# Norms pipelined by pairs of tiles in a two-block transformer kernel

## The reference

```python
# first block: mixer with adaLN, 32 experts of which each token takes 4
x = x + g1 * (mixed @ w_out)
h2 = rms_norm(x, norm2_g) * (1 + sc2) + sh2
x = x + g2 * moe_ffn(h2, ...)
x = rms_norm(x, final_g)
# second block, two layers
x = layer_norm_2(x, ln_emb_g, ln_emb_b)
for layer in range(2):
    mix = hybrid_mixer(x, ...)                      # attention + two-way retention
    x = layer_norm_2(ALPHA * x + mix, ln1_g[layer], ln1_b[layer])
    ffn = swiglu(x, ...) if layer == 0 else moe_swiglu(x, ...)   # 8 experts, 2 a token
    x = layer_norm_2(ALPHA * x + ffn, ln2_g[layer], ln2_b[layer])
```

## Time and profile before

| | us |
|---|---|
| median of 3 runs | 2596.67 (2596.26 to 2632.82) |
| the profiled execution | 2595.71 |
| its span | 2594.0 |
| PE busy | 2352.8 (91%) |
| DVE busy | 705.4 (27%) |
| ACT busy | 550.8 (21%) |
| POOL busy | 300.4 (12%) |

### The profile page before, as it was taken

How to read it: one execution, slowest core, us unless ns; L and a number is a source line. 1 busy time by engine, 2 the same in 40 slices (tenths; PEclk the granted TensorE clock), 3 DMA queues, 4 the chain that set the end, 5 groups by cost and what they waited for, 6 DMA issues and landing times.

```text
span 2594.0 us, 35046 instructions
## 1 busy us (share of the span) xinstructions
PE 2352.8 (91%) x13496; PEld 1499.8 (58%) x13497; DVE 705.4 (27%) x1313; ACT 550.8 (21%) x784; POOL 300.4 (12%) x129
## 2 busy tenths in 40 slices
PE   4999799999999999999949997999799869999996
PEld 3877644444444434444429876998698655444443
DVE  5854323222222222322251322010222331111013
ACT  1132011212112111111215811420266001111111
POOL 1000000000000000000017412660363000000000
PEclk8999889999999999999979988999899879999998
DMA  9942369999999999989924415444442436799560
GB/s 371 369 161 100 81 258 418 418 417 417 418 418 418 418 417 417 416 346 417 402 65 147 114 49 162 131 162 130 142 134 82 187 130 267 299 407 398 230 267 16
DMA packets 226021, 688.58 MB, mean 265 GB/s; under 512 B 31290, under 2 KB 120194, under 8 KB 190114
## 3 DMA queue, kind: packets, MB, share of 16 engines
q1 hardware_dynamic: 221472, 685.81, 69.0%
q10 hardware_dynamic: 4482, 1.81, 0.3%
HBM read 686.53 MB, written 1.05 MB: 265 GB/s over the span
## 4 chain that ended last, share of the span: by engine, by line
PE 72%; DMA 10%; SPq 8%; DVE 6%; issue 1%; ACT 1%; ACTq 0%; DVEq 0%
PE PS L876 15%; PE PS L624 13%; PE PS L633 11%; DMA RAW<-in_w_exp_in 9%; PE PS L977 7%; SPq L425 6%; PE PS L840 4%; PE PS L988 3%; PE PS L1156 3%; PE PS L673 2%; PE PS L859 2%; PE PS L941 2%; SPq L447 1%; PE PS L647 1%; PE PS L887 1%
## 5 line engine op out<-in xcount | busy, mean ns | idle before, releaser
L876 PE MATMUL PS<-RAW,Z 128*64 128x512 f32 x3168 | 715.0, 598 | 24.6 <-DMA RAW<-in_w_exp_in 23.8
L876 PEld LDWEIGHTS PS<-RAW,Z 128*64 128x64 f32 x3168 | 214.2, 137 | 456.1 <-issue 377.2
L377 POOL TENSOR_TENSOR WLO_D<-W,WHI_D 128x2048 fp32r<-128x2048 f32 x60 | 277.5, 4626 | 1364.3 <-ACT WHI_D L374 1364.3
L977 PE MATMUL PS<-W,Z 128*64 128x384 f32 (+1 forms) x1408 | 216.9, 465 | 7.4 <-DMA W<-in_moe_w 6.1
L633 PE MATMUL PS<-Z,W 128*128 128x256 f32 x768 | 177.0, 394 | 20.1 <-DVE Z L1980 12.3
L633 PEld LDWEIGHTS PS<-Z,W 128*128 128x128 f32 x768 | 151.6, 198 | 45.3 <-DVE Z L1980 13.8
L977 PEld LDWEIGHTS PS<-W,Z 128*64 128x64 f32 x1408 | 100.0, 138 | 125.4 <-issue 67.6
L624 PE MATMUL PS<-XHI,WHI_D 128*128 128x256 f32 x880 | 128.7, 290 | 29.2 <-ACT XHI L1353 19.5
L374 ACT ACTIVATE WHI_D<-W 128x2048 fp32r<-128x2048 f32 x60 | 114.1, 1904 | 177.0 <-DMA W<-in_w_in 91.5
L624 PEld LDWEIGHTS PS<-XHI,WHI_D 128*128 128x128 f32 x880 | 116.0, 196 | 37.6 <-ACT XHI L1353 20.3
L840 PE MATMUL PS<-Z 128*128 128x64 f32 x1088 | 128.6, 278 | 3.1 <-DVE Z L1763 3.1
(11 more groups left out here) (336 smaller groups left out, 2199.6 us busy)
## 6 DMA issues: line engine op xcount, KB each, us to landing
RAW<-in_w_exp_in SPq DMA_DIRECT2D x256, 1024.0 KB, 19.3
RAW<-in_w_exp_out SPq DMA_DIRECT2D x128, 1024.0 KB, 21.8
W<-in_moe_w SPq DMA_DIRECT2D x128, 704.0 KB, 15.1
W<-in_w_in SPq DMA_DIRECT2D x52, 1024.0 KB, 6.1
W<-in_moe_w SPq DMA_DIRECT2D x40, 1024.0 KB, 14.3
W<-in_ffn_w SPq DMA_DIRECT2D x33, 1024.0 KB, 5.3
W<-in_w_ada SPq DMA_DIRECT2D x24, 1024.0 KB, 13.0
W<-in_w_out SPq DMA_DIRECT2D x12, 1024.0 KB, 5.0
```

Of the source, the lines that this page charges most:

```text
L377: eng.tensor_tensor(lo, raw, hi.bitcast(F32), ALU.subtract).then_inc(sem("dense_lo"), 1)
L876: mm = pe.matmul(ps(bank, 512, 64 * h, 64 * h + 64), x, w[:, c:c + 512], start=first, stop=final, skip_group_check=True)
L977: mm = pe.matmul(ps(2 * i + b, n, 64 * h, 64 * h + 64), X1[:, s, :], first2(s)[:, c:c + n], start=(s == 0), stop=(s == 7), skip_group_chec ...
```

## The change

- **Layer norm in one pass by pairs** (`shift_sum`, `moments`, `normalised`, `shifted_parts`). The mean over the first 256 features is a shift that is taken off all tiles; then PE sums x and x^2 of each pair of tiles when DVE has it, and the variance is mean(x^2) - mean(x)^2. The sums of the first pairs stand between the jobs of `w_out`, or behind the last slot of ffn2. DVE scales by pairs, and ACT applies gain and bias with one instruction a tile, which writes XHI directly; then X again.
- **`first_jobs`**: the first two split jobs behind a norm do all work with XHI, tile by tile as pairs arrive, then all with XLO.
- **Final rms norm and embedding layer norm made one**: XW is X times final_g; its mean and variance and the sum of X^2 give one root, of var + EPS * mean(x^2) + EPS^2.
- **The ends of the experts**: X takes what Y holds before the last scatters, which go to different banks (`scatter_last`) and are added straight to X.
- **`route`**: logits and transposes alternate tile by tile as pairs arrive.
- **Head norm and mixed sum** by pairs; the product with the silu gate is put ahead of the wait for the head sums.
- **The output** is transposed, copied (by ACT and DVE) and stored in four pieces. The square root's table is loaded ahead (`root_table`), and the two expert stages share semaphores.

The core of the diff:

```diff
+            def first_jobs(lin):
+
+
+                n = ("qa0", "ffn1", "qa1").index(lin.name)
+
+                def split(q, buf):
+                    return buf[:, q % SPLIT_N, :].rearrange("p (k n) -> p k n", k=KT)
+
+                for s in range(2):
+                    q = split_ready(lin, s)
+                    job = lin.job0 + s
+                    bank_free(job)
+                    for k in range(KT):
+                        if s == 0 and k % 2 == 0:
+                            pe.wait_ge(sem("stream_hi"), 4 * n + k // 2 + 1)
+                        for j in range(2):
+                            for i, w in enumerate((WHI_D, WLO_D)):
+                                pe.matmul(ps(job % 2, T, c0=j * T), split(q, w)[:, k, j * P:(j + 1) * P], XHI[:, k, :],
+                                          start=(i == j == k == 0), stop=False, skip_group_check=True)
+                for s in range(2):
+                    q = split_ready(lin, s)
+                    job = lin.job0 + s
+                    for k in range(KT):
+                        if s == 0 and k % 2 == 0:
+                            pe.wait_ge(sem("stream_lo"), 4 * n + k // 2 + 1)
+                        for j in range(2):
+                            mm = pe.matmul(ps(job % 2, T, c0=j * T), split(q, WHI_D)[:, k, j * P:(j + 1) * P], XLO[:, k, :],
+                                           start=False, stop=(k == KT - 1), skip_group_check=True)
+                    mm.then_inc(sem("lin_done"), 1)
...
+            def shift_sum(src, b):
+
+                for k in range(2):
+                    mm = pe.matmul(ps(b, T), ONES[:, :], src[:, k, :], start=(k == 0), stop=(k == 1))
+                mm.then_inc(sem("norm_sum"), 1)
+
+            def moments(src, squares, p, first, last, b1, b2):
+
+
+                def total(bank, c0, x):
+                    for k in (2 * p, 2 * p + 1):
+                        mm = pe.matmul(ps(bank, T, c0=c0), ONES[:, :], x[:, k, :],
+                                       start=(first and k == 2 * p), stop=(last and k == 2 * p + 1))
+                    if last:
+                        mm.then_inc(sem("norm_sum"), 1)
+
+                norm[0] += 1
+                if not last:
+                    pe.wait_ge(sem("norm_in"), norm[0])
+                total(b1, 0, src)
+                pe.wait_ge(sem("norm_in"), norm[0])
+                total(b2, T, squares)
...
                 scatter(count, 0)
-                scatter(count, 1)
+                scatter_last("m1")
+                pe.wait_ge(sem("xw_ready"), 1)
+                shift_sum(XW[:, 0:2, :], 1)
+                for i, p in enumerate((0, 2, 1)):
+                    moments(XW, XWSQ, p, i == 0, False, 3, 1)
+                pe.wait_ge(sem("x_squared"), 1)
+                for k in range(KT):
+                    mm = pe.matmul(ps(0, T), ONES[:, :], H[:, k, :], start=(k == 0), stop=(k == KT - 1))
+                mm.then_inc(sem("norm_sum"), 1)
+                pe.wait_ge(sem("xw_shifted"), 1)
+                moments(XW, XWSQ, 3, False, True, 3, 1)
...
                 pe.wait_ge(sem("norm_in"), norm[0])
-                for k in range(KT):
-                    mm = pe.matmul(ps(4 + k // 2, T, c0=(k % 2) * T), SPREAD[:, k, :], SQ[0:16, 0:T], start=True, stop=True)
-                mm.then_inc(sem("norm_sum"), 1)
-                pe.wait_ge(sem("ret_out"), l + 1)
+                for b in (0, 2, 1, 3):
+                    for k in (2 * b, 2 * b + 1):
+                        mm = pe.matmul(ps(4 + b, T, c0=(k - 2 * b) * T), SPREAD[:, k, :], SQ[0:16, 0:T], start=True, stop=True)
+                    mm.then_inc(sem("norm_sum"), 1)
                 for s in range(2):
                     for part in range(2):
-                        feature_job(lins[f"wo_ret{l}"], s, z(QR, QR + 4), 4, part)
-                pe.wait_ge(sem("mix_ready"), l + 5)
+                        feature_job(lins[f"wo_ret{l}"], s, z(QR, QR + 4), 4, part,
+                                    ready=("ret_out", 2 * l + 1) if s == part == 0 else None)
+                lin = lins[f"w_out{l}"]
                 for s in range(4):
-                    feature_job(lins[f"w_out{l}"], s, z(G2A, G2A + 8))
-                layer_norm(X)
-                pe.wait_ge(sem("x2_ready"), 2 * l + 2)
+                    feature_job(lin, s, z(G2A, G2A + 8), ready=("mix_ready", 4 * l + 5) if s == 0 else None)
+                    if s == 1:
+                        pe.wait_ge(sem("evac_dve"), job_evac[lin.job0][1])
+                        shift_sum(X, 4)
+                    elif s == 2:
+                        moments(X, H, 0, True, False, 5, 4)
+                        moments(X, H, 1, False, False, 5, 4)
+                moments(X, H, 2, False, False, 5, 4)
+                pe.wait_ge(sem("evac_dve"), job_evac[lin.job0 + 3][1])
+                moments(X, H, 3, False, True, 5, 4)
 
             mixer2(0)
-            pe.wait_ge(sem("stream_hi"), 2)
-            for s in range(11):
+            first_jobs(lins["ffn1"])
...
+            def final_x(n, g, b, hi=True):
+
+
+                for p in range(4):
+                    act.wait_ge(sem("normed"), 4 * n + p + 1)
+                    for k in (2 * p, 2 * p + 1):
+                        a = act.activation((XHI if hi else X)[:, k, :], X[:, k, :], ACT.Identity,
+                                           bias=VEC[:, b + k:b + k + 1], scale=VEC[:, g + k:g + k + 1])
+                    a.then_inc(sem("stream_hi" if hi else "stream_x"), 1)
+                if hi:
+                    for p in range(4):
+                        for k in (2 * p, 2 * p + 1):
+                            a = act.activation(X[:, k, :], X[:, k, :], ACT.Identity,
+                                               bias=VEC[:, b + k:b + k + 1], scale=VEC[:, g + k:g + k + 1])
+                        a.then_inc(sem("stream_x"), 1)
 
...
-            root()
-            for q in range(2):
-                split_dense(act, q)
-            root()
-            stream_hi(1)
-            for q in range(2, SPLIT_N):
-                split_dense(act, q)
+            root_table()
+            split_dense(act, 0)
+            for i, p in enumerate((0, 2, 1, 3)):
+                act.wait_ge(sem("x_summed"), i + 1)
+                for k in (2 * p, 2 * p + 1):
+                    a = act.activation(XW[:, k, :], X[:, k, :], ACT.Identity, scale=VEC[:, V_FG + k:V_FG + k + 1])
+                a.then_inc(sem("xw_ready"), 1)
+            split_dense(act, 1)
+            for p in range(4):
+                a = act.activation(H[:, 2 * p:2 * p + 2, :], X[:, 2 * p:2 * p + 2, :], ACT.Square)
+            a.then_inc(sem("x_squared"), 1)
+            split_dense(act, 2)
+            norm_root(1)
+            final_x(1, V_EG, V_EB)
...
+            def normalised(x, b1, b2, order, rms_bank=None):
+
+
                 sums()
-                reciprocal_root([(SQ[:, 0:T], ps(4, T, c0=T))], n)
-                return dve.tensor_tensor(x, x, bc(SQ[:, 0:T], nk), ALU.mult)
-
-            def layer_norm(x, g, b, ready):
-                link(centre(x, KT, D))
-                affine(x, g, b).then_inc(sem(ready), 1)
+                link(dve.tensor_scalar(MEAN, ps(b1, T), 1.0 / D, None, ALU.mult))
+                link(dve.scalar_tensor_tensor(out=VAR, in0=MEAN, scalar=-1.0, in1=MEAN, op0=ALU.mult, op1=ALU.mult))
+                if rms_bank is not None:
+                    link(dve.scalar_tensor_tensor(out=VAR, in0=ps(rms_bank, T), scalar=EPS / D, in1=VAR, op0=ALU.mult, op1=ALU.add))
+                sums()
+                dve.scalar_tensor_tensor(out=VAR, in0=ps(b2, T, c0=T), scalar=1.0 / D, in1=VAR, op0=ALU.mult, op1=ALU.add)\
+                    .then_inc(sem("root_in"), 1)
+                dve.tensor_tensor(pair(x, order[0]), pair(x, order[0]), bc(MEAN, 2), ALU.subtract).then_inc(ch.sem, 1)
+                ch.n += 1
+                rt[0] += 1
+                dve.wait_ge(sem("root_out"), rt[0])
+                link(dve.reciprocal(ROOT, ROOT))
+                for p in order:
+                    if p != order[0]:
+                        link(dve.tensor_tensor(pair(x, p), pair(x, p), bc(MEAN, 2), ALU.subtract))
+                    dve.tensor_tensor(pair(X, p), pair(x, p), bc(ROOT, 2), ALU.mult).then_inc(sem("normed"), 1)
+
+            def stream_lo(n):
+
+                for p in range(4):
+                    dve.wait_ge(sem("stream_x"), 4 * n + p + 1)
+                    dve.tensor_tensor(pair(XLO, p), pair(X, p), pair(XHI, p).bitcast(F32), ALU.subtract)\
+                        .then_inc(sem("stream_lo"), 1)
...
+                dve.wait_ge(sem("m1_added"), count * 2 + 1)
+                for k in range(KT):
+                    i = dve.scalar_tensor_tensor(out=X[:, k, :], in0=Y[:, k, :], scalar=MOD[:, 40 + k:41 + k], in1=X[:, k, :],
+                                                 op0=ALU.mult, op1=ALU.add)
+                link(i)
+                for r in range(2):
```

(32 more changed lines are left out.)

373 lines of the change are left out of this document (217 added, 156 removed).

## The result

The changed kernel takes 2513.97 us (median of 4 executions, 2511.07 to 2518.45) where the kernel before takes 2596.5: a ratio of 0.965, with a 95% interval of 0.957 to 0.973, so faster by 3.5%. (The interval is wide because one of the four executions of the kernel before took 2632.82 us and the other three 2596.3 to 2596.7.) The forecast was 2506, with 2482 to 2530 as its range. The profiled execution took 2516.26 us, with a span of 2514.5 (before: 2594.0).

The account below looks back on a forecast made before the run. TensorE was busy 91% of the span, so only waits, about 241 us, could be won. Terms A to F summed to 90.0 us; 2595.7 less that gave 2505.7, as a median 2506, range 2482 to 2530.

Parts of the forecast that it names:

- B: End of the first experts to the mixer: 20 us won, 31 if undisturbed by GpSimd's weight splits.
- C: Mixer of layer 1 (head norm, mixed sum, layer norm): 19.7 us won, 25.5 without waits for weight splits.
- D: End of the feed-forward to the stream: 9.4 us won, 13.2 without waits for weight splits.
- E: Mixer of layer 2 to routing: 26.3 us won; no weights are split there.
- F: End of the kernel, last sums to the output's store: 11.3 us won.
- the lock: VectorE instructions with two SBUF inputs wait for GpSimd's whole weight splits; 3.8 us lost in the feed-forward's end.
- Rival 1: Two-input VectorE instructions are not held by weight splits: 111 us won, 2485; chance 0.22.
- Rival 2: More lost than counted, sums in pieces keeping the clock low, 3 us more in each norm: 2532; chance 0.19.
- Rival 3: The first expert loop begins when its weights come, so the first routing's 3.3 us would go: 2509; no separate chance.
- A: First rms norm to routing: 3.3 us won, at 1.84 us of PE a pair.
- Rival 4: Slower than before: interrupted sums leave PE at 1.2 GHz well into 60 split jobs, 2681 at half; chance 0.03.
- The tail: From a norm's last sum of squares to the first matmul using the result: 4.6 us with handovers.

Follow-up runs that it names:

- first run: The changed kernel once more, unchanged, on the chip of the next three runs: 2510.29 us, 0.9665 of the kernel before.
- third: Changed kernel plus 16 filler matmuls in PE's wait between a norm's last sum and what uses its result: 2504.92 us, 0.964 of the kernel before.
- eighth: Changed kernel plus GpSimd splits in four, filler matmuls, and the first two jobs behind a norm taking their XHI rows in turn, pair by pair: 2479.95 us.
- eleventh: The eighth run's kernel with the shift in PSUM besides and one filler in another bank: 2477.97 us, 0.9536 of the kernel before.
- sixth run: Changed kernel with both routings doing all transposes first and the logits behind them, instead of tile by tile in turn: 2505.85 us.
- after: The changed kernel's first trace, beside the kernel before: median 2513.97 us, profiled execution 2516.26 us.

## Why the prediction was right, and where it was off

**Direction, size and mechanism held.** Forecast 90.0 us, measured 82.5 by the first medians and 88.6 by those of the first run. The signs named ahead are there: subtractions and squares of 2.4 to 4.98 us in B, C and D, none in E and F, where every one of L1653, L2097 and L2100 took 0.69; waits of 4.69 us inside w_out of layer 1, none in layer 2. Two signs came only in part: a split of over 5 us shows once (5.03), so the lock fell on VectorE and hardly on GpSimd; and the stream matmuls came 4.9 us behind the last sum in C and D and 5.4 in B, not 4.6. Of the signs against it, a granted clock of 0.50 in the first stream jobs came for 3 to 6 us.

**Rival 1**, that two-input instructions are not held, is out by these rows and by the runs with pieces. Its 21 us of difference were about right as a price: pieces gave back 16.8, though with them VectorE is still held.

**Rival 2**, more lost to the clock, holds in part: the clock is low for about 6 us in B and C and 3.2 in D, and for both routings. But before, it was at 0.50 from 1622.5 to 1628.0 at this place as well, and the two jobs of the earlier trace rows hold that stretch, so the sum had it already. **Rival 3**, that the first loop takes A's gain back, is out: in the third, eighth and eleventh runs A is 4.4 to 4.5 us shorter than in the changed kernel, and from the logits to the last scatters it is 997.0, 996.9 and 996.4 us there against 996.2 and 996.1, so at most 0.9 of the 4.5 are lost. **Rival 4**, slower by a low clock through the stream, didn't come: from 1595.4 on the clock is 1.00.

**The terms.**
- *The start, 0 in the sum, -4.3 measured.* 3.7 of it are of the execution, not of the change; the half microsecond or more that is left stays open.
- *A, 3.3 in the sum, 1.0 measured.* The step that failed is "A pair costs PE (4.11 + 3.25)/4 = 1.84 us". The first pair came on time (300.1 forecast; 304.65 less the 4.31 of the start is 300.3). But a pair cost 2.35, as the clock stayed at 0.50, and the 4.11 of the price came from a stretch in which it had come back to 0.87 for the logits. The sixth run shows that the order did it there.
- *B, 20 in the sum, 20.2 measured.* The splits came where they were forecast (1314.2, 1319.2 and 1323.6 in after; less the 3.7 by which the experts end later, 1310.5, 1315.5 and 1320.0, against 1310.6, 1315.9 and 1321.0). The path of pair 0 did not: its square was to be done at 1316.5, ahead of the second split, and began 0.13 us behind it, so it was done at 1320.6 on that clock. That this cost nothing is luck: the sums end on pair 2, whose square was done at 1326.2 (forecast 1326.9), and they ended at 1338.2 (1339.3). The tail took 5.4 instead of 4.6. What the lock alone costs was counted as 11.5 and not measured by itself: with pieces B is 7.0 us shorter, with the shift in PSUM, filler and the first jobs in turn as well 10.9.
- *C, 19.7 in the sum, 16.7 measured.* The head norm and the mixed sum gave 12.2 instead of 12.7 where layer 2 shows them undisturbed (spread to the end of w_out without the sums in it, 59.98 before and 47.76 now). The lock is the mis-sized term: from spread to the end of w_out layer 1 takes 60.6 us and layer 2 takes 52.1. Of these 8.5 us 0.9 lie ahead of the shift's sum, so it is 7.6 and not the 5.8 that were taken off (4.8 and "1 for the clock"). The wait was right, 4.9 us from start to start. The clock behind it was not: 1.8 for the sums of pair 1 and 0.9 for the start of the last job.
- *D, 9.4 and 9.1.* The lock came as named (the square of pair 2 took 4.28 us, and PE waited 3.3 instead of 3.8), but the number is right because two errors cancel. From the end of ffn2 to the stream it is 17.1 us instead of 15.5, with the sums behind the wait at the low clock; the first two jobs then take 13.2 instead of 14.5, since the clock is low for 3.2 us and not for 5.5.
- *E, 26.3 in the sum, 23.5 measured.* The same step as in A: four pairs of 1.84 were 7.4, and 9.4 were measured. Here the order is not the cause, since it makes no gain when undone, but the low clock is: with filler E is 2.3 us shorter.
- *F, 11.3 and 12.5.* The four stores land faster than the one: from the last copy's end to the end of the span 3.1 us (2511.39 to 2514.5) against 4.5 (2589.50 to 2594.0). I had taken them as equal.
- *The tail, 4.6 in the sum.* From the last sum's end to the stream matmul it is 4.86 in C (1584.67 to 1589.53). The term that was too small is ACT's: 1.09 for two tiles instead of 0.85, which L1281 of the kernel before would have given. It didn't set the pace: a pair came every 1.33 us.
- *The loops.* -0.3 and 1.3 us. Over all eleven traces with the changed code the first loop differs by 1.6 us, so the first can't be told from nothing.
- *The range.* It was to leave out "the upper third" of the second rival's 2519 to 2544; above 2530 lies over half of it.

## What to carry to other kernels

When work of VectorE is cut up and moved under other work, look at what GpSimd runs there: an instruction that was safe in a quiet stretch can now wait for a whole one of GpSimd. Cut GpSimd's instruction, or put one of VectorE's two inputs into PSUM, but count how many instructions will take turns: eight multiplies in a row gained nothing from the cut, while eight of 0.69 us, with PE at work on each pair in between, gained 7 us. Such a price hangs on who starts first: 0.13 us decided whether a square took 0.69 or 4.94 us. Price matmuls behind a gap at the low clock for as long as they come in small portions with waits between, not at the pace of the same rows where they ran in one piece.

## What the runs showed of the hardware

- GpSimd and VectorE take turns by whole instructions: a subtraction of 0.69 us took up to 4.98, 2.83 and 1.75 us beside pieces of 4.60, 2.40 and 1.29. With one input in PSUM it is not held at all (0.67 to 0.69).
- A multiply by a column (128x256, one full input in SBUF) is held as well, 1.23 to 1.35 us each beside pieces.
- Busy at nearly all times, PE stayed at a granted clock of 0.50 for 9.4 us where small logits and transposes alternate; with the same matmuls in two blocks (the sixth run) the clock was back after about 4 us in the one routing, and not in 11 us in the other, where waits of 0.2 us lie between.
- Filler of ones by ones in a wait keeps the clock at 1.00 through it, but not always behind it: in two of five places it fell 1.2 and 1.8 us later. It gave 4.5 and 2.3 us in the routings, and 1.6 in front of a stream that waits for pairs.
- ACT with scale and bias as columns takes 0.59 us for 128x256 from SBUF to SBUF, with the scale alone as a column 0.49 (L1493), and a root of that size without either 0.42.
- The granted clock of the same code differs between executions: the sums of the last norm ran at 0.67 in one trace of the changed kernel and at 1.00 in another, 1.7 us apart.
